# Modulation vectors from unsplit f32 weights in column tiles, and the loops written out

## The chip, the core and the metric

One core of one Trainium2 chip runs the whole kernel. Its engines work side by side and meet at semaphores: TensorE (PE, matmuls; PEld is its weight load), VectorE (DVE), ScalarE (ACT), GpSimd (POOL) and SyncE (SP), which issues all DMAs of this kernel. The metric is the device time of one execution in microseconds (us), lower is better.

## The reference

A two-layer backbone on 256 tokens of `x` and 256 context tokens, width 1024, all in f32. Each layer is FFN, mixer (window attention and gated linear attention), FFN. Each of the three is scaled, shifted and gated by modulation vectors, nine per layer, which depend on the condition alone:

```python
def adaln(cond, w, b):
    m = (cond @ w + b)[..., None, :]
    return jnp.split(m, N_MOD, axis=-1)          # N_MOD = 9, w is 1024 x 9216 per layer
def modulate(h, shift, scale):
    return h * (1 + scale) + shift
def swiglu(h, w13, w2):
    up, gate = jnp.split(h @ w13, 2, axis=-1)
    return (jax.nn.silu(gate) * up) @ w2

cond = jax.nn.silu(c)
cond_ctx = jax.nn.silu(c_ctx)
xc = ctx
for l in range(DEPTH):                           # DEPTH = 2
    m = adaln(cond, w_mod[l], b_mod[l])
    mc = adaln(cond_ctx, w_mod[l], b_mod[l])
    x = x + 0.5 * m[2] * swiglu(modulate(rmsnorm(x, norm_w[l, 0]), m[0], m[1]), ffn1_w13[l], ffn1_w2[l])
    xc = xc + 0.5 * mc[2] * swiglu(modulate(rmsnorm(xc, norm_w[l, 0]), mc[0], mc[1]), ffn1_w13[l], ffn1_w2[l])
    ...                                          # the mixer with m[3], m[4], m[5]
    x = x + 0.5 * m[8] * swiglu(modulate(rmsnorm(x, norm_w[l, 2]), m[6], m[7]), ffn2_w13[l], ffn2_w2[l])
    ...                                          # the context the same, in layer 0 alone
return x
```

So `adaln` is a product of two condition vectors (`c` and `c_ctx`) with two matrices of 1024 x 9216: 72 MB of weights for two result rows.

## The kernel before

Activations lie transposed: 8 row tiles `kt` of 128 features, 512 tokens side by side (256 in the last FFN). TensorE's fast form takes f32 data whose low bits are cut off (F32R). To keep f32 accuracy every operand is split into a high and a low part, and each product is made of three matmuls: high by high, high by low, low by high (`mm3`, L1248 to L1250).

Weights come in units of 1 MB. For each unit SP loads `raw` (two slots), ACT casts it into `WH` (L513, two halves), DVE subtracts to get `WL` (L823, two halves; this is `prep` on either engine), and PE uses it. `raw`, `WH` and `WL` have two slots each, so the split of unit n+2 waits until PE is through with unit n (`half_done`). Units are numbered in one order for all engines (`schedule`), and each unit is 48 matmuls of 512 columns where it belongs to an FFN.

The modulation vectors go through the same stream of units: 72 units of 256 columns (`unit_mod`, L1298 and L1299: the stationary operand `cst` is 128 columns wide and holds silu(c) and silu(c_ctx) with their low parts in four of them, the moving one is `WH` or `WL`, 256 columns; 16 matmuls a unit). DVE copies the four rows to `mrow` (L849), PE turns them into columns and adds high and low parts in one (`mod_turn`, L1311, a small f32 matmul by `hilo`), and DVE adds the bias (L854). Eight of the units stand ahead of everything. The others are spread over the first three FFNs by `FFN_SEGMENTS`: in FFN 0 three iterations with 4 units each and eight with 2, in FFN 1 eleven with 2, in FFN 2 seven with 2 and four with none. An iteration is two FFN units (one pair of `w13` tiles each, 22 in an FFN), and each such segment is a hardware loop.

After the 22 units of an FFN's first half come 11 units of its second half (`ffn_out`), which need the last gated product. Ahead of each FFN stands a norm: ACT squares, PE sums by a plain f32 matmul with `ones` (L1333), POOL multiplies by `rstd` (L460), DVE scales and shifts (L907), ACT casts to `hH`, DVE makes `hL` (L899), and the first FFN unit takes the eight tiles as they come.

A matmul of plain f32 operands (L1311, L1333, L1486) is written once in the code and runs as two matmul instructions, so the trace counts two for each. The trace names the tiles by the program's names: `PS` is PSUM, `hidH` and `hidL` the hidden state of an FFN, `sg` the gated product.

Of the kernel before, what the change touches and what calls it, by code (L numbers as in the profile page):

```python
# [13 lines left out]
P = 128  # L23
# [24 lines left out]
MOD_UNITS = N_MOD * D // UW  # L48
MOD_FIRST = 8
PAIR_AT = 2  # L50
MOD_GROUP = 4

FFN_SEGMENTS = [[(3, 4), (8, 2)], [(11, 2)], [(7, 2), (4, 0)], [(11, 0)]]


def schedule():
# [7 lines left out]

    take("mod", MOD_FIRST)
    for l in range(DEPTH):
        for j in range(2):
            k = 2 * l + j
            if j == 1:
                take(("attn_proj", l), 6)  # L70
                take(("branch_a", l), 8)
                take(("gla_proj", l), 1 + 2 * (2 + 4))
                take(("branch_g", l), 8)
                take(("out", l), 4)
            for s, (iters, fill) in enumerate(FFN_SEGMENTS[k]):
                take(("ffn_in", k, s), iters * (2 + fill))
            take(("ffn_out", k), GROUPS)
# [5 lines left out]
N_UNITS = START["end"]  # L83


def hybrid_backbone(nc, a, out):

    ctx = ExitStack()
    with ctx:
# [13 lines left out]
        WL = sb("WL", [P, 2, UN], F32R)  # L103
        mod = sb("mod", [P, DEPTH * N_MOD * KT, 2])
# [20 lines left out]
        mrow = sb("mrow", [P, MOD_GROUP, UW])  # L125
        rstd = mrow[:, 2:4, :].rearrange("p a c -> p (a c)")
# [62 lines left out]
        cst_hi = sem("cst_hi")  # L189
        cst_ready = sem("cst_ready")  # L190
# [4 lines left out]
        hilo_ready = sem("hilo_ready")  # L195
# [88 lines left out]
        wmod_d = [a["w_mod"][l].rearrange("(k p) c -> p k c", p=P) for l in range(DEPTH)]  # L284
# [60 lines left out]
        def _(sp):  # L345
# [10 lines left out]
            def load(n, slot, view, shape, pair=0):  # L356


                if pair == 0 and not (isinstance(n, int) and n < 2):
                    sp.wait_ge(lo_ready, 2 * n - 2)  # L360
                if pair == 1:
                    sp.wait_ge(lo_ready, 2 * n)
                dst = raw[:, slot, :].rearrange("p (k c) -> p k c", k=shape)
                sp.dma_start(dst, view).then_inc(raw_in[slot], 16)

            def load_pair(n, slot, f, view, at):

                sp.wait_ge(lo_ready, 2 * n - 2)
                dst = raw[:, slot, :].rearrange("p (k e c) -> p e k c", k=KT, e=2)
                sp.dma_start(dst[:, 0], view[:, :, 0:D_FF][:, :, bass.ds(at, P)]).then_inc(raw_in[slot], 16)  # L370
                sp.dma_start(dst[:, 1], view[:, :, D_FF:2 * D_FF][:, :, bass.ds(at, P)]).then_inc(gate_in[f], 16)

            load(0, 0, wmod_d[0][:, :, 0:UW], KT)
            load(1, 1, wmod_d[0][:, :, UW:2 * UW], KT)

# [7 lines left out]
            with sp.Fori(1, MOD_FIRST // 2) as i:  # L383
                for s in range(2):
                    load(2 * i + s, s, wmod_d[0][:, :, bass.ds(sp.snap((2 * i + s) * UW), UW)], KT)
# [9 lines left out]
            for k in range(4):  # L395
                l = k // 2
                if k % 2 == 1:
                    n = START[("attn_proj", l)]
                    cols = [COL["av"], COL["ak"]] + [COL["aq"] + j * UW for j in range(4)]
                    for j, c in enumerate(cols):  # L400
                        load(n + j, (n + j) % 2, win_d[l][:, :, c:c + UW], KT)
                    n = START[("branch_a", l)]
                    with sp.Fori(0, 4) as i:
                        load(n + 2 * i, n % 2, win_d[l][:, :, bass.ds(sp.snap(COL["ga"] + i * UW), UW)], KT, 1)
                        load(n + 2 * i + 1, (n + 1) % 2, wba_d[l][:, :, bass.ds(sp.snap(i * UW), UW)], KT, 2)
# [7 lines left out]
                    for j, c in enumerate(cols):  # L413
                        load(n + j, (n + j) % 2, win_d[l][:, :, c:c + UW], KT)
                    n = START[("branch_g", l)]
                    with sp.Fori(0, 4) as i:
                        load(n + 2 * i, n % 2, win_d[l][:, :, bass.ds(sp.snap(COL["gg"] + i * UW), UW)], KT, 1)
                        load(n + 2 * i + 1, (n + 1) % 2, wbg_d[l][:, :, bass.ds(sp.snap(i * UW), UW)], KT, 2)
                    n = START[("out", l)]
                    with sp.Fori(0, 2) as i:  # L420
                        for s in range(2):
                            load(n + 2 * i + s, (n + s) % 2, wout_d[l][:, :, bass.ds(sp.snap((2 * i + s) * UW), UW)], KT)
                g0 = 0
# [1244 lines left out]
```

## Time and profile before

| what | us |
|---|---|
| median of 3 runs (lowest to highest) | 2851.77 (2848.77 to 2857.4) |
| span of the profiled execution | 2850.1 |
| PE busy | 2542.8 (89%) |
| PEld busy | 2140.0 (75%) |
| DVE busy | 1278.3 (45%) |
| ACT busy | 1010.5 (35%) |
| POOL busy | 263.1 (9%) |
| mean granted TensorE clock | 0.958 of full |

A matmul's recorded time includes its way through the array, so neighbours overlap in the record; the distance from one start to the next is what it costs. 301.2 MB are moved. Times in the rows are us from the start of the span.

### The profile page before, as it was taken

The numbers are of one execution on the slowest core, as the hardware profiler recorded it, in microseconds if no ns is written. First come the engines' busy times: TensorE is split into PE (matmuls) and PEld (weight loads), VectorE is DVE, ScalarE is ACT, GpSimd is POOL, SyncE is SP. The second block draws the span as 40 slices with busy tenths as digits, with TensorE's granted clock in tenths as the row PEclk, the third lists the DMA queues.
The fourth block names the chain that finished last, engine by engine and source line by source line (L and its number), as shares of the span: only waits on it lengthen the run. The fifth ranks groups of instructions, "written<-read, shape, count | busy, mean of one in ns | idle before, by whom it ended". The sixth has DMA issues, their size and how long they took to land.

```text
span 2850.1 us, 34522 instructions
## 1 busy us (share of the span) xinstructions
PE 2542.8 (89%) x13357; PEld 2140.0 (75%) x13357; DVE 1278.3 (45%) x1675; ACT 1010.5 (35%) x1361; POOL 263.1 (9%) x296
## 2 busy tenths in 40 slices
PE   5999999896898887979999998999998788879999
PEld 4778778684777675857788786878786687779998
DVE  4544441436425544345444325443314654555554
ACT  3433331234324443233333213333213544454442
POOL 2000000100004533010000001000001002430000
PEclk8999999898999998989999999999998999999999
DMA  5554442120131101314444322444321142215564
GB/s 193 170 155 145 149 134 102 59 74 1 59 109 40 47 28 59 103 59 132 147 147 147 118 91 86 147 147 118 98 93 59 45 134 74 74 35 172 148 187 136
DMA packets 353492, 301.21 MB, mean 106 GB/s; under 512 B 6368, under 2 KB 341192, under 8 KB 353416
## 3 DMA queue, kind: packets, MB, share of 16 engines
q1 hardware_dynamic: 353416, 300.18, 34.3%
q8 instruction: 50, 0.82, 0.1%
q14 instruction: 26, 0.21, 0.0%
HBM read 299.10 MB, written 1.05 MB: 105 GB/s over the span
## 4 chain that ended last, share of the span: by engine, by line
PE 71%; DVE 12%; issue 6%; ACT 6%; POOL 3%; DMA 1%; SPq 0%; ACTq 0%; DVEq 0%; POOLq 0%
PE PS L1248 22%; PE PS L1250 20%; PE PS L1249 20%; DVE WL L823 4%; ACT WH L513 2%; DVE sq L907 2%; PE PS L1575 1%; PE PS L1311 1%; PE PS L1333 1%; POOL dq L469 1%; DVE hL L899 1%; PE PS L1536 1%; POOL dq L484 1%; DVE small L1039 1%; ACT dq L732 1%
## 5 line engine op out<-in xcount | busy, mean ns | idle before, releaser
L823 DVE TENSOR_TENSOR WL<-raw,WH 128x1024 fp32r<-128x1024 f32 x564 | 680.8, 1248 | 883.9 <-ACT WH L513 882.3
L513 ACT CAST WH<-raw 128x1024 fp32r<-128x1024 f32 x564 | 562.2, 1046 | 913.8 <-PE PS L1250 848.3
L1248 PE MATMUL PS<-hH,WH 128*128 128x512 f32 (+1 forms) x2096 | 780.7, 372 | 82.4 <-DVE WL L823 57.1
L1250 PE MATMUL PS<-hH,WL 128*128 128x512 f32 (+1 forms) x2096 | 758.1, 362 | 0.0
L1249 PE MATMUL PS<-hL,WH 128*128 128x512 f32 (+1 forms) x2096 | 758.1, 362 | 0.0
L1248 PEld LDWEIGHTS PS<-hH,WH 128*128 128x128 f32 x2096 | 402.8, 192 | 165.9 <-DVE WL L823 69.1
L1250 PEld LDWEIGHTS PS<-hH,WL 128*128 128x128 f32 x2096 | 403.3, 192 | 59.5
L1249 PEld LDWEIGHTS PS<-hL,WH 128*128 128x128 f32 x2096 | 404.1, 193 | 53.9 <-issue 1.0
L1248 PE MATMUL PS<-hidH,WH 128*128 (+2 forms) x704 | 260.0, 369 | 5.2 <-DVE sg L961 5.2
L1249 PE MATMUL PS<-hidL,WH 128*128 (+2 forms) x704 | 257.9, 366 | 0.0
L1250 PE MATMUL PS<-hidH,WL 128*128 (+2 forms) x704 | 257.0, 365 | 0.0
L460 POOL TENSOR_TENSOR sq<-xT,mrow 128x512 f32<-128x512 f32 (+1 forms) x48 | 65.9, 1407 | 1675.9 <-ACT mrow L547 1675.9
L1298 PE MATMUL PS<-WH,cst 128*128 128x256 f32 x576 | 149.5, 295 | 11.5 <-DVE WL L823 10.1
L1248 PEld LDWEIGHTS PS<-hidH,WH 128*128 128x128 f32 x704 | 132.0, 188 | 30.3 <-DVE sg L961 6.6
L1250 PEld LDWEIGHTS PS<-hidH,WL 128*128 128x128 f32 x704 | 132.6, 188 | 25.2
L1249 PEld LDWEIGHTS PS<-hidL,WH 128*128 128x128 f32 x704 | 132.2, 188 | 23.1
L1299 PE MATMUL PS<-WL,cst 128*128 128x256 f32 x576 | 145.4, 289 | 0.0
L1248 PE MATMUL PS<-actH,WH 128*128 128x512 f32 (+1 forms) x384 | 130.9, 341 | 13.5 <-DVE actL L1209 13.5
L1250 PE MATMUL PS<-actH,WL 128*128 128x512 f32 (+1 forms) x384 | 131.9, 343 | 0.0
L1249 PE MATMUL PS<-actL,WH 128*128 128x512 f32 (+1 forms) x384 | 131.3, 342 | 0.0
L1298 PEld LDWEIGHTS PS<-WH,cst 128*128 128x128 f32 x576 | 113.2, 197 | 18.3 <-DVE WL L823 13.3
L1283 PE MATMUL PS<-WH,hH 128*128 128x256 f32 x320 | 97.5, 305 | 26.0 <-DVE hL L899 26.0
(175 smaller groups left out, 2733.9 us busy)
## 6 DMA issues: line engine op xcount, KB each, us to landing
raw<-in_ffn_w SPq DMA_DIRECT2D x176, 512.0 KB, 4.6
raw<-in_w_mod SPq DMA_DIRECT2D x72, 1024.0 KB, 5.0
raw<-in_w_in SPq DMA_DIRECT2D x54, 1024.0 KB, 5.3
raw<-in_ffn_w SPq DMA_DIRECT2D x44, 1024.0 KB, 5.0
raw<-in_w_branch_attn SPq DMA_DIRECT2D x8, 1024.0 KB, 7.8
raw<-in_w_branch_gla SPq DMA_DIRECT2D x8, 1024.0 KB, 7.7
raw<-in_w_out SPq DMA_DIRECT2D x8, 1024.0 KB, 5.2
xin<-in_x SPq DMA_DIRECT2D x1, 1024.0 KB, 9.9
```

The lines of the kernel that those rows point to most:

```text
L460: nc.gpsimd.tensor_tensor(sq[:, kt, 0:T], xT[:, kt, 0:T], rstd[:, 0:T], ALU.mult).then_inc(xn_done, 1)
L469: ins = nc.gpsimd.tensor_tensor(dq[:, 0, d, :].rearrange("p (n m) -> p n m", m=P), b[:, :, at:at + 1].to_broadcast([P, NTB, P]), b, ALU.su ...
L484: nc.gpsimd.tensor_tensor(ov[:, 0, :, 0, :], fm, bv[:, 0, :, 0, :], ALU.subtract)
L513: nc.scalar.copy(half(WH, par, e, rows), half(raw, par, e, rows)).then_inc(hi_ready, 1)
L823: nc.vector.tensor_tensor(half(WL, par, e, rows), half(raw, par, e, rows), half(WH, par, e, rows).bitcast(F32), ALU.subtract).then_inc(lo_ ...
L907: ins = nc.vector.tensor_scalar(sq[:, kt, c * S:(c + 1) * S], sq[:, kt, c * S:(c + 1) * S], coefA[:, kt, c:c + 1], shift[:, kt, c:c + 1], ...
L1248: mm(o, wh, ah, start=start, stop=False)
L1249: mm(o, wh, al, start=False, stop=False)
L1250: return mm(o, wl, ah, start=False, stop=stop)
L1283: mm(o, ah, wh[:, kt, :], start=kt == 0, stop=False)
L1298: mm(PS[:, 4 + f, 0:UW], cst[:, kt, :], wh[:, kt, :], start=kt == 0, stop=False)
L1299: ins = mm(PS[:, 4 + f, 0:UW], cst[:, kt, :], wl[:, kt, :], start=False, stop=kt == KT - 1)
```

## The change

The modulation weights no longer pass through `raw`, `WH` and `WL`. They have two slots of their own (`mraw`, 128 x 2048), each filled by a row tile of 128 weight rows and 2048 columns (1 MB, a "piece", 72 in all; eight pieces, one for each `kt`, make a "set" of 2048 modulation values, nine sets). A piece is four plain f32 matmuls of 512 columns (`mod_piece`): the stationary operand is `cst[:, kt, :]`, 32 columns wide, and the result of column block j goes to PSUM partitions 32j to 32j+31, so each matmul uses another fourth of the array's columns. After eight pieces DVE copies the whole bank once (128 x 512) and PE turns it by four transposes; DVE adds the bias for 16 columns at once. Set 0 stands ahead of FFN 0. FFN 0 takes sets 1 to 3, FFN 1 sets 4 and 5, FFN 2 sets 6 to 8, a piece at a time between half units. Set 4 reaches over both layers and needs two DMAs a piece. `rstd` gets its own buffer. All hardware loops are written out, on all engines; the unit numbers become constants. Splits of the first pair of FFN 0 come ahead of the `kt` loop of the norm, those of FFN 1 to 3 in the stage before.

```diff
-FFN_SEGMENTS = [[(3, 4), (8, 2)], [(11, 2)], [(7, 2), (4, 0)], [(11, 0)]]
+MW = 2048
+MOD_SETS = DEPTH * N_MOD * D // MW
+MOD_Q = 4
+MOD_M = 32
+SETS_IN_FFN = [(1, 3), (4, 2), (6, 3), (9, 0)]
...
+def mod_places(k):
+
+    first, sets = SETS_IN_FFN[k]
+    places = {}
+    for i in range(KT * sets):
+        places.setdefault(i * (2 * FT - 3) // (KT * sets - 1), []).append(KT * first + i)
+    return places
...
+        mraw = sb("mraw", [P, 2, MW])
...
-        cst = sb("cst", [P, KT, P], F32R)
-        hilo = sb("hilo", [4, 2])
+        cst = sb("cst", [P, KT, MOD_M])
...
+            def load_mod(p):
+
+                kt, w = p % KT, MW // MOD_Q
+                if p >= 2:
+                    sp.wait_ge(mod_mm, p - 1)
+                for l in range(DEPTH):
+                    own = [(j, c) for j, (of, c) in enumerate(MOD_D[p]) if of == l]
+                    if own:
+                        (j0, c0), n = own[0], len(own)
+                        sp.dma_start(mraw[:, p % 2, j0 * w:(j0 + n) * w],
+                                     a["w_mod"][l][kt * P:(kt + 1) * P, c0 * w:(c0 + n) * w]).then_inc(mraw_in[p % 2], 16)
...
+            for p in range(2, KT):
+                load_mod(p)
+                if p >= KT - 2:
+                    f = p - KT + 2
+                    load_pair(START[("ffn_in", 0)] + f, f, w13_d[0])
...
+                for f in range(FT + 2):
+                    if f < FT:
+                        if k or f >= 2:
+                            load_pair(n + f, f, w13_d[k])
+                    else:
+                        load(w2 + f - FT, w2_d[k][:, 2 * (f - FT):2 * (f - FT) + 2, :], 2)
+                    if f >= 2:
+                        for at in (2 * f - 4, 2 * f - 3):
+                            for p in places.get(at, ()):
+                                load_mod(p)
...
+            def mod_rows(u):
+
+                dve.wait_ge(mod_mm, KT * (u + 1))
+                nc.vector.tensor_copy(mrow[:], PS[:, 4, :]).then_inc(mod_row, 1)
...
-            def unit_mod(n, f, par):
-
-                wh, wl = weights(par)
-                for e in range(2):
-                    pe.wait_ge(lo_ready, 2 * n + e + 1)
-                    for kt in range(e * KT // 2, (e + 1) * KT // 2):
-                        mm(PS[:, 4 + f, 0:UW], cst[:, kt, :], wh[:, kt, :], start=kt == 0, stop=False)
-                        ins = mm(PS[:, 4 + f, 0:UW], cst[:, kt, :], wl[:, kt, :], start=False, stop=kt == KT - 1)
-                    ins.then_inc(half_done, 1)
+            def mod_piece(p):
+
+                u, kt = divmod(p, KT)
+                w = MW // MOD_Q
+                pe.wait_ge(mraw_in[p % 2], mod_in(p))
+                if kt == 0 and u:
+                    pe.wait_ge(mod_row, u)
+                for j in range(MOD_Q):
+                    ins = mm(PS[j * MOD_M:(j + 1) * MOD_M, 4, 0:w], cst[:, kt, :], mraw[:, p % 2, j * w:(j + 1) * w],
+                             start=kt == 0, stop=kt == KT - 1)
+                ins.then_inc(mod_mm, 1)
...
+            def mod_turn(u):
+
+                pe.wait_ge(mod_row, u + 1)
+                if u:
+                    pe.wait_ge(mod_done, u)
+                for q in range(MW // MOD_Q // P):
+                    ins = nc.tensor.transpose(PS[:, 5, q * P:(q + 1) * P], mrow[:, q * P:(q + 1) * P], ident[:])
                 ins.then_inc(mod_t, 1)
...
-                    with pe.Fori(0, iters) as i:
...
+                for f in range(FT):
+                    if f > 1:
+                        pe.wait_ge((gated_a, gated_b)[f % 2], g0 + f // 2)
+                    unit_cols(n + f, 2 + f % 2, hH, hL, T, step=-2, h0=KT * ffn_norm(k) if f == 0 else None,
+                              between=[nothing] * 3 + [lambda: mods_at(2 * f)] + [nothing] * 3)
+                    mods_at(2 * f + 1)
+                    if f - 1 in ends:
+                        mod_turn(ends[f - 1])
...
-                pe.wait_ge(mod_done, GROUPS0[(k + 1, 0)] if k < 3 else GROUPS0["end"])
...
+                pe.wait_ge(mod_done, sum(SETS_IN_FFN[k]))
```

PE at the start of the program. `xin` is the input, `ident` and `ones` are constants. Before, the loop of the first modulation units follows the norm's sums:

```order
L1328 MATMUL PS<-ident,xin 128x128 x32
L1333 MATMUL PS<-sq,ones 128x512 x8
L1342 UNCONDITIONAL_BRANCH
L1296 ISA
L1298 MATMUL PS<-WH,cst 128x256
L1299 MATMUL PS<-WL,cst 128x256
```

Now:

```order
L1230 MATMUL PS<-ident,xin 128x128 x32
L1235 MATMUL PS<-sq,ones 128x512 x8
L1200 MATMUL PS<-mraw,cst 32x512 x32
L1213 MATMUL PS<-ident,mrow 128x128 x4
L1150 MATMUL PS<-hH,WH 128x512
```

The eight pieces of set 0 are 32 matmuls in a row, and the first FFN unit follows the transposes.

SP at the same place, behind the small constants. Before, the loop of modulation units, with two of them and the two halves of a pair in the FFN's loop:

```order
L382 DMA negsink<-in_attn_sink 128x16
L383 UNCONDITIONAL_BRANCH
L383 ISA
L364 ISA
L364 DMA raw<-in_w_mod 128x8x256
```

Now:

```order
L390 DMA negsink<-in_attn_sink 128x16
L378 DMA mraw<-in_w_mod 128x2048 x5
L366 DMA raw<-in_ffn_w 128x8x128
L367 DMA raw<-in_ffn_w 128x8x128
L378 DMA mraw<-in_w_mod 128x2048
L366 DMA raw<-in_ffn_w 128x8x128
L367 DMA raw<-in_ffn_w 128x8x128
```

The first pair of `w13` is issued behind the load of piece 6, and the last piece of set 0 behind that pair.

DVE at the end of FFN 0's first half. Before:

```order
L954 TENSOR_TENSOR sg<-sg,PS 128x512
L854 TENSOR_TENSOR mod<-PS,bmodT 128x8
L823 TENSOR_TENSOR WL<-raw,WH 128x1024 x2
L961 TENSOR_TENSOR sg<-sg,PS 128x512
L963 TENSOR_TENSOR hidL<-sg,hidH 128x1024
```

Now:

```order
L797 COPY mrow<-PS 128x512
L776 TENSOR_TENSOR WL<-raw,WH 128x1024 x2
L873 TENSOR_TENSOR sg<-sg,PS 128x512
L875 TENSOR_TENSOR hidL<-sg,hidH 128x1024
L803 TENSOR_TENSOR mod<-PS,bmodT 128x32
L776 TENSOR_TENSOR WL<-raw,WH 128x1024 x20
```

The last bias addition of the FFN moved behind the last gated product and its low part; `ffn_out` on PE waits for it.

## Rows read from the trace of the kernel before

**Rows 1.** The page: engines, and the chain that ended last

```profile
PE 2542.8 (89%) x13357; PEld 2140.0 (75%) x13357; DVE 1278.3 (45%) x1675; ACT 1010.5 (35%) x1361; POOL 263.1 (9%) x296
PE 71%; DVE 12%; issue 6%; ACT 6%; POOL 3%; DMA 1%; SPq 0%; ACTq 0%; DVEq 0%; POOLq 0%
```

**Rows 2.** Stretches: length, then busy us (instructions) by engine, PE clock, DMA

```profile
core 0: us, PE busy (x) PEld busy (x) DVE busy (x) ACT busy (x) POOL busy (x), PEclk, DMA share, GB/s
...
82.08:420.92 338.84, 319.26 (x1585) 264.43 (x1585) 157.29 (x187) 120.65 (x136) 0.00 (x0) 0.98 0.50 152
...
1272.39:1284.80 12.41, 2.45 (x18) 2.01 (x17) 9.00 (x7) 4.45 (x6) 10.37 (x8) 0.72 0.00 0
1284.80:1301.54 16.74, 14.35 (x48) 9.92 (x49) 13.03 (x23) 7.00 (x9) 1.08 (x1) 0.80 0.27 75
1272.39:1603.11 330.72, 304.67 (x1499) 251.75 (x1497) 153.85 (x177) 114.76 (x132) 11.46 (x8) 0.98 0.46 140
1732.87:2036.52 303.65, 282.30 (x1339) 232.70 (x1337) 132.58 (x149) 99.60 (x116) 11.45 (x8) 0.98 0.42 124
219.75:248.29 28.54, 27.36 (x137) 22.82 (x136) 12.54 (x14) 9.82 (x11) 0.00 (x0) 1.00 0.49 147
116.61:151.05 34.44, 32.92 (x177) 27.73 (x176) 17.84 (x20) 13.98 (x15) 0.00 (x0) 1.00 0.60 183
1939.61:2034.95 95.34, 95.34 (x421) 78.75 (x420) 31.36 (x31) 24.13 (x28) 0.00 (x0) 1.00 0.36 106
```

**Rows 3.** Timeline of PE, one modulation unit in FFN 0: start, us, instruction

```profile
219.51 0.40 PE L1250 MATMUL PS<-hH,WL 128*128 128x512 f32 x1
219.75 0.28 PE L1298 MATMUL PS<-WH,cst 128*128 128x256 f32 x1
219.87 0.28 PE L1299 MATMUL PS<-WL,cst 128*128 128x256 f32 x1
...
222.39 0.50 PE L1248 MATMUL PS<-hH,WH 128*128 128x512 f32 x1 [0.59 <-DVE WL L823]
```

**Rows 4.** Timelines of PE: plain f32 matmuls, the first with all columns, then row tiles

```profile
23.40 7.03 PE L1333 MATMUL PS<-sq,ones 128*128 128x512 f32 x16
...
6.29 0.30 PE L1320 MATMUL PS<-ident,rows 24*128 24x24 f32 x1
6.29 0.28 PE L1321 MATMUL PS<-ident,rows 16*128 16x16 f32 x1
...
851.73 0.39 PE L1250 MATMUL PS<-hH,WL 128*128 128x512 f32 x1
852.05 1.98 PE L1486 MATMUL PS<-lrT,gw 32*128 32x512 f32 x4
853.96 0.50 PE L1248 MATMUL PS<-hH,WH 128*128 128x512 f32 x1
```

**Rows 5.** Timeline of PEld in the norm's sums: weight loads of plain f32 matmuls

```profile
23.84 0.19 PEld L1333 LDWEIGHTS PS<-sq,ones 128*128 128x128 f32 x1 [0.24 <-ACT sq L543]
24.26 0.19 PEld L1333 LDWEIGHTS PS<-sq,ones 128*128 128x128 f32 x1 [0.24 <-issue]
```

**Rows 6.** The start: waits from 0 to 82 us; first FFN matmul; transposes; a PSUM copy

```profile
ACT WH L513 <- DMA raw<-in_w_mod: 20.2, 6, 6.3
...
82.08 0.50 PE L1248 MATMUL PS<-hH,WH 128*128 128x512 f32 x1 [0.75 <-DVE WL L823]
...
18.18 5.38 PE L1328 MATMUL PS<-ident,xin 128*128 128x128 f32 x32 [11.60 <-DMA xin<-in_ctx]
...
19.34 0.69 DVE L840 COPY xT<-PS 128x512 f32<-128x512 f32 x1 [5.87 <-PE PS L1328]
```

**Rows 7.** DMA: the page's queue row, and issues with KB and us to landing

```profile
q1 hardware_dynamic: 353416, 300.18, 34.3%
...
raw<-in_w_mod SPq DMA_DIRECT2D x72, 1024.0 KB, 5.0
```

**Rows 8.** Timelines of PE and DVE from FFN 0's first half to `ffn_out`

```profile
419.12 0.39 PE L1250 MATMUL PS<-hH,WL 128*128 128x512 f32 x1
420.92 0.49 PE L1248 MATMUL PS<-hidH,WH 128*128 128x512 f32 x1 [1.41 <-DVE sg L961]
...
420.18 0.69 DVE L961 TENSOR_TENSOR sg<-sg,PS 128x512 f32<-128x512 f32 x1 [6.58 <-ACT sg L590]
421.98 1.23 DVE L963 TENSOR_TENSOR hidL<-sg,hidH 128x1024 fp32r<-128x1024 f32 x1 [1.11 <-ACT hidH L592]
```

**Rows 9.** Timeline of PE: a norm with no modulation unit behind its sums

```profile
544.22 7.03 PE L1333 MATMUL PS<-sq,ones 128*128 128x512 f32 x16
560.97 0.55 PE L1283 MATMUL PS<-WH,hH 128*128 128x256 f32 x1 [9.73 <-DVE hL L899]
```

More of the change, by code:

```diff
@@ L437, in _ @@
-                n = START[("ffn_out", k)]
-                with sp.Fori(0, GROUPS // 2) as i:
-                    for s in range(2):
-                        load(n + 2 * i + s, (n + s) % 2, w2_d[k][:, bass.ds(sp.snap((2 * i + s) * 2), 2), :], 2)
-                load(n + GROUPS - 1, (n + GROUPS - 1) % 2, w2_d[k][:, FT - 2:FT, :], 2)
+                    for j in range(4):
+                        load(n + j, wout_d[l][:, :, j * UW:(j + 1) * UW])
+                n, places = START[("ffn_in", k)], mod_places(k)
@@ L443, in _ @@
+                for g in range(2, GROUPS):
+                    load(w2 + g, w2_d[k][:, 2 * g:2 * g + 2, :], 2)
             sp.wait_ge(out_ready, 2)
@@ new lines, in ffn @@
+                n = START[("ffn_in", k)]
+                for i in range(GROUPS):
+                    u, g = n + 2 * i, g0 + i
+                    prep(u + 1)
+                    act.wait_ge(half_done, 2 * (u + 1))
+                    if g:
+                        act.wait_ge(hid_lo, g)
+                    nc.scalar.activation(sg[:, 0, 0:T], PS[:, 0, 0:T], ACT.Silu).then_inc(silu_done, 1)
+                    prep(u + 2, rows=i == GROUPS - 1)
+                    act.wait_ge(half_done, 2 * (u + 2))
+                    nc.scalar.activation(sg[:, 1, 0:T], PS[:, 1, 0:T], ACT.Silu).then_inc(silu_done, 1)
+                    act.wait_ge(gated_b, g + 1)
+                    nc.scalar.copy(hidH[:, 2 * i:2 * i + 2, 0:T], sg[:, :, 0:T]).then_inc(hid_hi, 1)
@@ L604, in ffn @@
                 n = START[("ffn_out", k)]
-                with act.Fori(0, GROUPS // 2) as i:
-                    for s in range(2):
-                        prep(n + 2 * i + s + 1, (n + s + 1) % 2, rows=True)
-                prep(n + GROUPS, (n + GROUPS) % 2, rows=k == 1)
+                for g in range(GROUPS):
+                    prep(n + g + 1, rows=g < GROUPS - 1)
             def qk_tiles(l, j):
@@ L683, in branch @@
                 nc.scalar.preload_act_table(ACT.Sigmoid)
[L684 to L685 removed]
+                for i in range(4):
+                    prep(n + 2 * i + 1)
                     act.wait_ge(half_done, 2 * (n + 2 * i + 1))
```

442 lines of the change are left out of this document (141 added, 301 removed).

## The prediction

> **What bounds the kernel now.** I read the page first: PE is busy for 89% of the span and holds 71% of the chain that ended last, DVE and ACT are busy for 45% and 35% [rows 1]. So time goes where PE's own stream gets shorter or longer, and work taken from DVE and ACT counts only where PE waits for it. Then I cut the span into stretches [rows 2]. The last four iterations of FFN 2 carry no modulation unit: 420 matmuls of 512 columns in 95.3 us, 0.227 each, so an FFN unit of 48 costs 10.9 and an iteration of two 21.8. An iteration with two modulation units takes 28.54 and one with four 34.44. The two units of the first therefore cost 6.7: each is 16 matmuls at 0.12 (1.9), then PE stands 0.6 for the low part of the next weights, because a modulation unit is shorter on PE than its successor's split on ACT and DVE; from the first of the 16 to the next FFN matmul it is 2.64 [rows 3]. Twice 2.64 and a turn of 1.06 and the loop's end make up the rest. The start is bound otherwise: the first FFN matmul comes at 82.08, and until there ACT waits 20.2 us for modulation weights [rows 6].
>
> **The change, by stretches.** Modulation touches PE in four places: the start, and FFN 0, 1 and 2. Of the profiled execution these are 0 to 420.92, 1272.39 to 1603.11 and 1732.87 to 2036.52, each up to the first matmul of `ffn_out` [rows 2, 8]: 420.9 + 330.7 + 303.7 = 1055.3 us. I build the same three anew, with c for what one piece costs PE.
>
> *The price c of a piece.* It is four plain f32 matmuls of 512 columns. Such a matmul shows as two instructions, and 16 of them take 7.03 us: 0.43 each, 0.86 for one matmul as written [rows 4]. No row shows column tiles. The bounds:
> Serial, all eight instructions one after the other: 8 x 0.43 = 3.44.
> All four tiles side by side: two instructions deep, 0.86.
> Between them: rows show that different tiles of the array can run together, since L1320 and L1321, in row tiles at rows 64 and 0, start within the same 0.01 us [rows 4]. But the instructions come tile by tile, and the second of a tile cannot stream before its first is through; if PE starts matmuls in program order, the first instruction of tile j+1 starts with the second of tile j, and the piece takes five slots: 5 x 0.43 = 2.15.
> Weight loads lie under the preceding matmul: 0.19 in a slot of 0.43, with 0.24 idle [rows 5]. Changing the tile shape costs extra: four instructions in a 32-row tile take 852.05 to 853.96, 1.91 for 1.72 of streaming, and start 0.1 late [rows 4]; with the slow second matmul behind it I take 0.4 a piece.
> So c is 1.3, 2.55 or 3.84. I take the middle one, rounded to 2.6, since the rows that are nearest (L1320, L1321) show tiles together and every row shows PE starting in order. That is the decisive choice of this prediction: 64 pieces lie in the FFNs, and each 0.1 us of c is 6.4 us.
>
> The Trainium skill, "TensorE: Matmul & The Clock Gate", section "Part 3: Packing small matmuls — row/col tiling", gives 2.38 times the speed for three column tiles and says that matmuls start and end strictly in program order. The first figure alone would carry over as about 0.8 of full overlap, an estimate by that page of 1.1 us a piece and some 2711 us in all; the second is the reason for five slots. The same section says that a weight load overlaps a running matmul only where the row groups differ, which all four tiles here share. The trace speaks against that for full tiles [rows 5], and no run so far shows it for column tiles; it is the fourth case below.
>
> *Start.* PE sums the norm until 30.3 (23.40 and 16 slots of 0.43) [rows 4]. Pieces 0 and 1 have landed by then and run to 35.5. The other six go through two slots: a load of 1 MB lands 5.0 us after issue [rows 7], so a round of two pieces takes about 5.0 + 2.6 + 0.5, and three rounds with the last piece end near 59. The pair of FFN 0 is issued between pieces 6 and 7; the queue moved 300 MB in 34.3% of the span, 3.4 us per MB [rows 7], so piece 7 ends near 62. Then in a chain: copy of the bank 0.7 (L840 has the same shape) [rows 6], four transposes 0.7 (32 took 5.38), bias and coefficients 0.5, DVE's split of the first pair 2.4, and scale, cast and low part of the first tile with their semaphores 3. First FFN matmul at 70, against 82.1; bounds 62 (loads fully side by side) and 78.
>
> *First unit of an FFN.* It takes the eight tiles as they come, partly at the lower clock: 16.7 us in FFN 1 (1284.80 to 1301.54, clock 0.80) [rows 2]. I keep 16.7 for all three; between 14 and 20.
>
> *Norm ahead of FFN 1 and 2.* 12.4 us from the end of the sums to the first matmul, with a modulation unit on PE inside and the split of a modulation unit on DVE in front of the scaling [rows 2]. Without either it is like the norm of the mixer: sums start at 544.22, the last of 16 starts 15 x 0.43 later, at 550.7, and the first matmul comes at 560.97, 10.3 later [rows 9]. Saves 2.1 each.
>
> *Stream.* 21 units x 10.9 = 228.9 in each FFN. The 2.64 and 1.06 of the old units are gone. In their place 24c, 16c and 24c, and turns of 0.7 inside the stream (2, 1 and 2). A piece follows its set's DVE copy where it begins the next set: the copy comes up to 4.9 us after a unit's end, the piece 5.5 after it, so it is just covered; if not, 1 us a set.
>
> *Into `ffn_out`.* Now PE resumes 1.8 us after its last matmul started, released by the gated product [rows 8]. The bias addition now stands behind the cast and the low part, which ends at 423.21, and PE waits for it: 4.5 instead of 1.8. I add 2 for the clock, since a pause of that length can bring half rate for a stretch. Between 2.5 and 9 an FFN.
>
> *Covered at nothing:* the 1 MB loads of pieces inside the FFNs (a piece is issued about 1.5 units, 15 us, ahead; a landing takes 5.0; the DMA share was 0.36 to 0.60 in those stretches [rows 2] and the bytes stay the same); SP's in-order wait for a piece's slot ahead of the next pair (the piece two before is done a unit earlier); 72 splits fewer on ACT and DVE; the loops written out. That last has one exposed piece, at most 2 us in all: branches at loops' ends in the mixer. FFN 3, the mixers and the `ffn_out` parts are as before.
>
> *Sum,* in us: FFN 0 with the start: 70 + 16.7 + 228.9 + 1.4 + 4.5 + 2 + 24 x 2.6 = 385.9. FFN 1: 10.3 + 16.7 + 228.9 + 0.7 + 4.5 + 2 + 16 x 2.6 = 304.7. FFN 2: 10.3 + 16.7 + 228.9 + 1.4 + 4.5 + 2 + 24 x 2.6 = 326.2. Together 1016.8 against 1055.3: 38.5 less. FFN 0 gains 35, FFN 1 26, and FFN 2 loses 22, since it carries 24 pieces where 14 units stood. Span 2850.1 - 38.5 = 2811.6; the median of the runs is 1.7 above the profiled span, so 2813. In general the gain is 275 less the start less 64c; even is reached at c = 3.2.
>
> **Rivals.**
> *All four tiles together,* c = 1.3, start at 65: gain 127, 2725 us. For it: tiles that start in the same 0.01 us [rows 4]. Against it: two instructions of one tile stand next to each other in the stream.
> *Serial,* c = 3.84, start at 75: 46 us slower, 2898. It decides as soon as a column tile's matmul waits for the one before it, for instance because f32 operands in two instructions, or another input path of the array, don't allow two streams. For it: no row shows two matmuls of 512 columns side by side. It loses although nothing stalls: 64 x 3.84 is 246 us of PE for what cost some 215 with its waits.
> *Serial with open weight loads,* each instruction 0.43 + 0.19: c = 5.4, start at 82, about 3000.
> *The new waits eat the gain:* c = 2.6, but each DVE copy, each bias addition and each pause costs its upper bound: 9 sets x 1, 3 x 4.5 more, first units at 20, start at 78: 40 us back, 2853, no change.
>
> **Numbers.** A change under 0.3%, 9 us, can't be told from none. Five slots 0.47, around 2813 with its own range 2785 to 2840 (c from 2.3 to 2.9, and the start). All together 0.20, serial 0.22, serial with open loads 0.04, waits eat the gain 0.07. Faster by over 0.3% (under 2843): 0.20 + 0.45 = 0.65; same 0.08; slower 0.27. The range takes in the all-together and the serial case, 2715 to 2905.
>
> **What would show it.** In the trace after, four matmul groups on `mraw`: starts of the eight instructions of a piece at 0, 0.43, 0.43, 0.86, 0.86 and so on for five slots, pairwise for all together, 0.43 apart throughout for serial. From the last FFN matmul before a piece to the first one behind it: 2.6 + 0.2. First FFN matmul near 70. `ffn_out` released by the bias addition after 4.5, three times. FFN 2 longer than before by 22. An idle PE ahead of pieces, released by the load of `mraw`, would show my cover for the loads wrong; one ahead of FFN matmuls with no releaser would put it on the written-out code.

## The result, and the profile after

| | before | changed | ratio |
|---|---|---|---|
| median, us | 2850.81 (2848.77 to 2857.4) | 2703.19 (2699.01 to 2704.76) | 0.947 (95% interval 0.9458 to 0.9481) |
| profiled span, us | 2850.1 | 2702.8 | |

147.6 us less, where 38 less was forecast: outside the range, whose lower end was 2715. It is the case "all four tiles together" (2725) and some 20 us more.

The page of the changed kernel, engines and chain:

```profile
PE 2427.4 (90%) x12529; PEld 1976.6 (73%) x12529; DVE 1088.5 (40%) x1444; ACT 871.4 (32%) x1216; POOL 253.1 (9%) x296
PE 76%; DVE 10%; issue 6%; ACT 4%; POOL 3%; DMA 1%; SPq 0%; DVEq 0%; POOLq 0%; ACTq 0%
```

PE has 115 us less to do and was nearly as large a share of the span before [rows 1]: the kernel is still bound there, and its own stream got shorter. DVE and ACT have 190 and 139 us less, which hardly counts by itself.

Stretches of the changed kernel (columns as in [rows 2]): the start; FFN 0 from its first matmul to `ffn_out`; FFN 1 and FFN 2 from the end of the norm's sums to `ffn_out`; 90 us of `ffn_out`.

```profile
0.00:64.41 64.41, 28.06 (x122) 11.36 (x122) 12.04 (x25) 12.25 (x17) 11.28 (x16) 0.77 0.63 217
64.41:341.83 277.42, 273.39 (x1260) 202.38 (x1261) 89.67 (x103) 72.90 (x86) 0.00 (x0) 0.99 0.54 178
1187.74:1467.33 279.59, 264.34 (x1194) 201.58 (x1193) 97.88 (x106) 75.45 (x90) 10.52 (x8) 0.98 0.44 139
1595.19:1884.80 289.61, 274.42 (x1263) 202.13 (x1261) 98.48 (x108) 75.45 (x90) 10.52 (x8) 0.98 0.49 160
350.00:440.00 90.00, 90.00 (x399) 74.53 (x398) 18.88 (x16) 16.03 (x16) 0.00 (x0) 1.00 0.28 94
```

The three stretches of the sum are now 64.4 + 277.4 + 279.6 + 289.6 = 911.0 against 1055.3: 144.3 of the 147.3 us between the two spans. FFN 0 with the start gained 79.1, FFN 1 51.1 and FFN 2 14.0, which the forecast had losing 22.

Now the piece itself. Timelines of PE: three narrow windows on the first piece (each row groups the instructions that are under way in the window; its first number is the first start, the last the count), then a piece between FFN matmuls, and under it the weight loads (PEld) there.

```profile
29.55 0.64 PE L1200 MATMUL PS<-mraw,cst 128*32 128x512 f32 x4
...
29.55 1.07 PE L1200 MATMUL PS<-mraw,cst 128*32 128x512 f32 x8
...
30.00 1.04 PE L1200 MATMUL PS<-mraw,cst 128*32 128x512 f32 x8
...
73.16 0.40 PE L1152 MATMUL PS<-hH,WL 128*128 128x512 f32 x1
73.48 1.06 PE L1200 MATMUL PS<-mraw,cst 128*32 128x512 f32 x8
74.48 0.50 PE L1150 MATMUL PS<-hH,WH 128*128 128x512 f32 x1
...
73.48 0.16 PEld L1200 LDWEIGHTS PS<-mraw,cst 128*32 128x32 f32 x8 [0.37 <-issue]
```

Four instructions start at 29.55, in the window 29.54 to 29.70, and four more from 30.00 on; the next piece follows at 30.43. So it is pairs in four tiles: two slots of 0.43 for eight instructions, 0.88 a piece, where one plain matmul alone already takes 0.86 [rows 4]. The four starts of a slot lie 7 ns apart. The rows do not name the tile of an instruction; that one of each tile starts at once is read from the number four and from the run with one tile, below, where no two instructions start together. All eight weight loads lie within 0.16 us, under the first slot. In the stream PE goes from its last FFN matmul to the next in 1.32 us. That is 1.09 beside the matmul's own 0.227, and the 48 matmuls behind a piece begin a little slower. A whole period is the safest measure: with one piece to a unit of 48, PE resumes at 93.29 and again at 105.39.

```profile
93.29 0.50 PE L1150 MATMUL PS<-hH,WH 128*128 128x512 f32 x1
...
105.39 0.50 PE L1150 MATMUL PS<-hH,WH 128*128 128x512 f32 x1
```

12.10 less 48 x 0.227 gives c = 1.20: the number to set against the forecast's 2.6.

The start, and the step into `ffn_out` (timelines of PE, then of DVE):

```profile
35.55 1.08 PE L1200 MATMUL PS<-mraw,cst 128*32 128x512 f32 x4 [4.08 <-DMA mraw<-in_w_mod]
...
36.41 1.08 PE L1200 MATMUL PS<-mraw,cst 128*32 128x512 f32 x4
...
55.54 1.93 PE L1200 MATMUL PS<-mraw,cst 128*32 128x512 f32 x8 [4.15 <-DMA mraw<-in_w_mod]
58.29 1.12 PE L1213 MATMUL PS<-ident,mrow 128*128 128x128 f32 x4 [0.81 <-DVE mrow L797]
64.41 0.77 PE L1150 MATMUL PS<-hH,WH 128*128 128x512 f32 x1 [5.00 <-DVE hL L826]
...
337.55 0.39 PE L1152 MATMUL PS<-hH,WL 128*128 128x512 f32 x1
337.78 0.60 PE L1213 MATMUL PS<-ident,mrow 128*128 128x128 f32 x4
341.83 0.64 PE L1150 MATMUL PS<-hidH,WH 128*128 128x512 f32 x1 [3.46 <-issue]
...
338.61 0.69 DVE L873 TENSOR_TENSOR sg<-sg,PS 128x512 f32<-128x512 f32 x1 [8.55 <-ACT sg L556]
340.40 1.23 DVE L875 TENSOR_TENSOR hidL<-sg,hidH 128x1024 fp32r<-128x1024 f32 x1 [1.11 <-ACT hidH L558]
341.55 0.18 DVE L803 TENSOR_TENSOR mod<-PS,bmodT 128x32 f32<-128x32 f32 x1
```

Two stretches of the same start (columns as in [rows 2]), and what PE waits for on pieces, up to 65 us and in the whole kernel (us in total, times, longest):

```profile
35.50:57.50 22.00, 11.61 (x48) 1.22 (x48) 0.00 (x0) 1.99 (x2) 5.41 (x5) 0.50 0.93 311
57.50:64.41 6.91, 1.12 (x5) 0.75 (x5) 5.55 (x11) 1.24 (x2) 0.00 (x0) 0.50 0.22 56
...
PE PS L1200 <- DMA mraw<-in_w_mod: 14.4, 6, 4.2
...
PE PS L1200 <- DMA mraw<-in_w_mod: 14.7, 7, 4.2
```

At the start PE waits for the load of each of pieces 2 to 7, and these six run at a granted clock of 0.50: the second four instructions of a piece start 0.86 behind the first four (35.55 and 36.41), not 0.43, so a piece takes 1.7 us there. Inside the FFNs the loads are covered, as forecast: 14.4 of the 14.7 us of waits stand at the start.

Into `ffn_out` PE resumes 4.28 us after its last FFN matmul, against 1.80 [rows 8], in the order that the forecast gave: gated product, cast, low part (L875), bias (L803, ends at 341.73), and then PE. The trace names no releaser there, only "issue"; that it is the bias addition is read from the 0.1 us between the two rows and borne out by the run without it below.

### The profile page after: what moved, and what is told of

Same layout as the page of the kernel before. It is cut to its first block, busy times and chain, and to the rows that moved or that the text cites. A ratio compares the mean times of both kernels' runs of the same rounds, so it can differ in the third digit from the quotient of the medians.

```text
span 2702.8 us, 29281 instructions
## 1 busy us (share of the span) xinstructions
PE 2427.4 (90%) x12529; PEld 1976.6 (73%) x12529; DVE 1088.5 (40%) x1444; ACT 871.4 (32%) x1216; POOL 253.1 (9%) x296
## 4 chain that ended last, share of the span: by engine, by line
PE 76%; DVE 10%; issue 6%; ACT 4%; POOL 3%; DMA 1%; SPq 0%; DVEq 0%; POOLq 0%; ACTq 0%
PE PS L1150 22%; PE PS L1151 22%; PE PS L1152 22%; PE PS L1200 3%; DVE sq L833 2%; PE PS L1458 1%; PE PS L1235 1%; POOL dq L473 1%; DVE hL L826 1%; DMA mraw<-in_w_mod 1%; DVE WL L776 1%; PE PS L1419 1%; DVE small L941 1%; ACT dq L685 1%; POOL dq L488 1%
## 5 line engine op out<-in xcount | busy, mean ns | idle before, releaser
L776 DVE TENSOR_TENSOR WL<-raw,WH 128x1024 fp32r<-128x1024 f32 x420 | 502.7, 1238 | 531.4 <-ACT WH L516 530.7
L516 ACT CAST WH<-raw 128x1024 fp32r<-128x1024 f32 x420 | 418.9, 1046 | 457.2 <-PE PS L1152 417.3
L1150 PE MATMUL PS<-hidH,WH 128*128 128x512 f32 (+1 forms) x704 | 257.5, 366 | 11.3 <-issue 10.4
L1151 PE MATMUL PS<-hidL,WH 128*128 128x512 f32 (+1 forms) x704 | 257.3, 365 | 0.0
L1152 PE MATMUL PS<-hidH,WL 128*128 128x512 f32 (+1 forms) x704 | 257.0, 365 | 0.0
L464 POOL TENSOR_TENSOR sq<-xT,rstd 128x512 f32<-128x512 f32 (+1 forms) x48 | 57.9, 1240 | 1533.3 <-ACT rstd L533 1533.3
L873 DVE TENSOR_TENSOR sg<-sg,PS 128x512 f32<-128x512 f32 (+1 forms) x44 | 27.3, 621 | 314.5 <-ACT sg L556 314.5
L556 ACT ACTIVATE sg<-PS 128x512 f32<-128x512 f32 (+1 forms) x44 | 23.9, 544 | 354.1 <-PE PS L1152 354.1
L869 DVE TENSOR_TENSOR sg<-sg,PS 128x512 f32<-128x512 f32 (+1 forms) x44 | 27.3, 620 | 231.4 <-ACT sg L553 231.4
```

What stands on the lines that cost most here:

```text
L464: nc.gpsimd.tensor_tensor(sq[:, kt, 0:T], xT[:, kt, 0:T], rstd[:, 0:T], ALU.mult).then_inc(xn_done, 1)
L516: nc.scalar.copy(half(WH, n % 2, e, rows), half(raw, n % 2, e, rows)).then_inc(hi_ready, 1)
L776: nc.vector.tensor_tensor(half(WL, n % 2, e, rows), half(raw, n % 2, e, rows), half(WH, n % 2, e, rows).bitcast(F32), ALU.subtract).then_i ...
L869: nc.vector.tensor_tensor(sg[:, 0, 0:T], sg[:, 0, 0:T], PS[:, 2, 0:T], ALU.mult).then_inc(gated_a, 1)
L873: nc.vector.tensor_tensor(sg[:, 1, 0:T], sg[:, 1, 0:T], PS[:, 3, 0:T], ALU.mult).then_inc(gated_b, 1)
L1150: mm(o, wh, ah, start=start, stop=False)
```

## Experiments

Periods and c below are read as above, from one PE resumption behind a piece to the next, with 48 FFN matmuls between them. The kernel before was timed anew beside each group of runs, with medians of 2854.8, 2854.0 and 2854.7; the ratios are to those. The changed kernel was not timed again. Its 2703.2 stands beside a 2850.8 of the kernel before, so differences to it in microseconds are sure to some 4 us only.

**One column tile for all four.** The four matmuls of a piece write the same 32 partitions, into one sum; three quarters of the modulation vectors get no sum of their own.

```
-  mm(PS[j * MOD_M:(j + 1) * MOD_M, 4, 0:w], ...
+  mm(PS[0:MOD_M, 4, 0:w], ...
```

> The changed kernel with one edit: all four matmuls of a piece write PSUM partitions 0 to 31, so they share one column tile instead of having one each. Instructions, shapes and bytes are the same; the modulation vectors come out wrong (the four column blocks are added up). Theory (the four column tiles stream side by side, and that alone makes a piece cheap): the eight instructions run one after the other, 8 x 0.43 = 3.44 a piece, some 2.55 more than now; 64 pieces in the FFNs make 163 us, the eight at the start some 12 of which the loads hide a part: 2870 to 2885 in all, slower than the kernel before. Rival (a piece is cheap because it needs no split and no wait, the tiles matter little): under 2760.

Measured 2871.09 us (2869.2 to 2871.96), ratio 1.0054 (1.0038 to 1.0071): slower than before the change. PE, the first two instructions of a piece, and a period:

```profile
82.86 0.62 PE L1200 MATMUL PS<-mraw,cst 128*32 128x512 f32 x1
...
83.32 0.59 PE L1200 MATMUL PS<-mraw,cst 128*32 128x512 f32 x1
...
124.94 0.50 PE L1150 MATMUL PS<-hH,WH 128*128 128x512 f32 x1
...
139.59 0.50 PE L1150 MATMUL PS<-hH,WH 128*128 128x512 f32 x1
```

The instructions start one by one. 14.65 less 10.90 is c = 3.75, the serial case of the forecast (3.84). With the same 72 pieces, transfers, waits and written-out loops the kernel is 16 us slower than before when the tiles don't run side by side, and 147 faster when they do. The column tiles are worth 168 us (2871.1 - 2703.2), more than the whole gain.

**Halves, tile by tile.** Each of the four matmuls is cut into two of 256 columns that stand next to each other in the program, in the same tile.

```
   for j in range(MOD_Q):
+      for e in range(2):
+          ... columns e * w // 2 to (e + 1) * w // 2 of tile j
```

> The changed kernel with each of a piece's four matmuls cut into two of 256 columns, written tile by tile: both of tile 0, both of tile 1, and so on. 16 instructions a piece instead of 8, the same columns in all. Theory A (TensorE doesn't hold a tile's matmul back for one of another tile that is still waiting, whatever the program order): a piece stays near 0.9 plus 0.2, the whole within 10 us of the changed kernel, 2703 to 2713. Theory B (matmuls start in program order, and only the two passes of one f32 matmul are taken apart): tile j+1 starts with the second half of tile j, five slots of 0.43, about 2.15 plus 0.2 a piece, 1.2 x 64 = 80 us more: about 2783.

Measured 2703.37 us (2700.35 to 2705.47), ratio 0.947 (0.9454 to 0.9486): the same as the changed kernel. The window 30.25 to 30.35 and a period:

```profile
30.26 0.44 PE L1201 MATMUL PS<-mraw,cst 128*32 128x256 f32 x4
...
82.07 0.50 PE L1150 MATMUL PS<-hH,WH 128*128 128x512 f32 x1
...
94.23 0.50 PE L1150 MATMUL PS<-hH,WH 128*128 128x512 f32 x1
```

Each tile now has four instructions of its own in a row, and still one of each of the four tiles starts at once; c is 1.26. A tile's second instruction, as the kernel writes them, therefore does not hold back another tile's first. (Whether PE itself takes them out of the written order, or they reach it so, no row shows.) That ends "five slots": with order kept, this form would have taken 13 slots of 0.22, 2.8 us.

**Only one of the four matmuls,** in all pieces but the first of each set.

```
   for j in range(MOD_Q):
+      if j and kt:
+          continue
```

> The changed kernel, where in 63 of the 72 pieces (all but the first of each set) only the first of the four matmuls stands, and the other three column tiles get nothing; three quarters of the modulation vectors are then wrong from there on, and every transfer, wait and turn stands as it was. 56 of the 64 pieces in the FFN stretches are cut so. Theory A (the four column tiles run beside each other, and three of the four matmuls cost only their issue, some 7 ns each in the trace of the changed kernel): 1 us less, 2702 us (2699 to 2704). Theory B (the four share the engine, so that each is a quarter of the 0.86 us): 56 x 0.65 = 36 us less, 2667.

Measured 2699.1 us (2692.98 to 2699.47), ratio 0.9452 (0.9436 to 0.9468). PE resumes at 124.00 and 136.09: c = 1.19 with one matmul, 1.20 with four.

```profile
124.00 0.50 PE L1150 MATMUL PS<-hH,WH 128*128 128x512 f32 x1
...
136.09 0.50 PE L1150 MATMUL PS<-hH,WH 128*128 128x512 f32 x1
```

The period gives 0.6 us in all for the three left out. The 4 us of the medians are more than that, and not explained by it. How far traces differ where nothing was edited shows in the second layer's mixer. This run leaves it as the changed kernel has it, and the change altered only its loops and where its buffers lie. From the last of its norm's sums to the first of the next norm's, in the kernel before, the changed kernel and this one:

```profile
2166.25:2637.25 471.00, 389.29 (x2578) 353.49 (x2577) 255.67 (x397) 211.71 (x336) 84.85 (x128) 0.93 0.28 86
...
2012.64:2489.82 477.18, 397.61 (x2578) 358.78 (x2577) 255.66 (x397) 210.86 (x336) 88.38 (x128) 0.91 0.27 85
...
2012.00:2479.12 467.12, 392.19 (x2578) 356.96 (x2577) 255.53 (x397) 210.73 (x336) 83.81 (x128) 0.92 0.28 87
```

Of the 11.6 us between the profiled runs of the last two, 10.1 stand there. The 36 us of "each a quarter" are excluded.

**Every piece's four matmuls twice.**

```
+  for r in range(2):
       for j in range(MOD_Q):
```

> The changed kernel, where each piece issues its four matmuls twice in a row, into the same sums (the modulation vectors come out twice as large). In the changed kernel a piece makes the stream of FFN matmuls 1.09 us longer, of which two passes of 512 columns are 0.88 us by the pieces that follow one another at the start. Theory A (1.09 is 0.88 for the passes, paid again, and 0.21 for going over to the other shape and back, paid once): 64 x 0.88 = 56 us more, 2759 us (2755 to 2763), and the gap in the stream is 2.2 us a piece. Theory B (the 1.09 goes with each set of four): 64 x 1.09 = 70 us more, 2773.

Measured 2759.03 us (2755.79 to 2759.21), ratio 0.9658 (0.964 to 0.9675); 56 us more, as the first theory had it. The period:

```profile
131.00 0.50 PE L1150 MATMUL PS<-hH,WH 128*128 128x512 f32 x1
...
144.00 0.50 PE L1150 MATMUL PS<-hH,WH 128*128 128x512 f32 x1
```

13.00, c = 2.10. The second set costs 0.90, so 0.3 of the 1.20 goes to changing the shape and back and is paid once, however many matmuls stand in the piece. Two pieces in one place would save some 0.3 us, 32 such pairs 10 us; that was not run.

**The kernel before, with its loops written out.** Only every loop of the program was unrolled, with constants as addresses and wait values.

```
-  with pe.Fori(0, iters) as i:
+  for i in range(0, iters):
```

> The kernel before with all its hardware loops written out on all engines, and nothing else changed: the modulation units are split and interleaved as before. Theory (the loops' share is what the two traces show outside the modulation): ffn_out's matmuls at 0.227 instead of 0.233, 3 x 3.5 us, and 5 us at the branch loops' ends and in their matmuls, 1 us more in the last FFN: 16 to 20 us less than before, 2831 to 2835. Rival 1 (written-out code costs nothing and gives nothing, as forecast): 2849 to 2851. Rival 2 (the 0.6 us stands ahead of FFN units were the loops' register work, not the splits): 30 us or more less.

Measured 2857.88 us (2854.05 to 2863.41), ratio 1.0011 (1.0001 to 1.0022). The theory fell: written-out loops give nothing. That agrees with the forecast's "at most 2 us", but it left a question open, since `ffn_out`, which the change does not touch, ran faster. Stretches of 90 us in `ffn_out`, of the kernel before and of this one:

```profile
440.00:530.00 90.00, 90.00 (x388) 72.39 (x387) 18.90 (x16) 16.00 (x16) 0.00 (x0) 1.00 0.28 95
...
440.00:530.00 90.00, 90.00 (x387) 72.41 (x386) 18.88 (x16) 16.01 (x16) 0.00 (x0) 1.00 0.28 96
```

388 and 387 matmuls of 512 columns in 90 us, 0.232 each, at full clock in all; the changed kernel has 399, 0.226 each (first block of rows after). Loops don't explain it.

**Where the buffers lie.** In the kernel before, `hidH`, `hidL`, `actH` and `actL` begin 32 bytes off a multiple of 64 in each partition, by the sizes of the buffers ahead of them; the change drops and adds other buffers ahead of them, and they now begin at a multiple of 64. One run moves them back in the changed kernel, the other moves them down in the kernel before.

```
+  pad = sb("pad", [P, 8])
   with ExitStack() as r:
       below_sq = ...
```

> The changed kernel with 32 unused bytes ahead of hidH, hidL, actH and actL, which then begin 32 bytes off a multiple of 64, as in the kernel before. Theory A: the pitch in ffn_out rises from 227 to 231-237 ns and the time by 14 us to 2717 (2713 to 2721); then some 14 us of the 148 gained come from where the buffers lie and 134 from the column tiles and what goes with them. Theory B: 2703 as before.

Measured 2712.81 us (2707.8 to 2714.83), ratio 0.9499 (0.9476 to 0.9521): 9.6 more than the changed kernel, or 8 by the ratios. Its `ffn_out`, then that of the other run:

```profile
350.00:440.00 90.00, 90.00 (x387) 72.29 (x386) 18.88 (x16) 16.02 (x16) 0.00 (x0) 1.00 0.26 86
...
440.00:530.00 90.00, 90.00 (x395) 73.86 (x394) 20.94 (x18) 17.99 (x18) 0.00 (x0) 1.00 0.28 93
```

```
-  hilo = sb("hilo", [4, 2])
-  epsc = sb("epsc", [P, 2])
+  epsc = sb("epsc", [P, 4])
+  hilo = epsc[0:4, 2:4]
```

> The kernel before, with the two numbers of hilo put into free room of epsc, so that every buffer behind lies 32 bytes lower: hidH, hidL, actH and actL then begin at multiples of 64 bytes as in the changed kernel, where they began 32 bytes off in the kernel before. Theory A (a plain 256-column matmul reads its moving operand 5 to 9 ns slower when it begins 32 bytes off): 1582 matmuls with hid by 6.5 ns and 578 with act by 6.5 ns, together 14 us, so 2837 us (2833 to 2841), and the pitch in ffn_out falls from 231-237 to 227 ns. Theory B (the pitch comes from something else that the change brought, such as the loops or the traffic of the queue): the pitch stays at 231 to 237 ns and the time at 2851 (2848 to 2855).

Measured 2843.42 us (2837.22 to 2849.39), ratio 0.996 (0.9948 to 0.9973): 11 us less than before, from where a buffer of 8 bytes stands. 32 empty bytes bring 399 matmuls down to 387; taking them out of the kernel before brings 388 up to 395, not to 399. So the address is shown to be a cause. It is worth some 10 us of the 147, where 14 were expected from the pitch (the distance from one start to the next); 9.6 and 11 carry an uncertainty of some 4 us each, and the firm evidence is the pitch. What keeps the last 4 in 90 us is open: in that kernel matmuls of the first kind (`hidH` with `WH`) are still 231 ns apart from the next, the other two kinds 228.

**The last piece of an FFN one unit earlier.** The pieces of a stage are spread over two half units fewer, so that copy, transposes and bias lie under the last unit.

```
-  places.setdefault(i * (2 * FT - 3) // (KT * sets - 1), [])
+  places.setdefault(i * (2 * FT - 5) // (KT * sets - 1), [])
```

> The changed kernel with the pieces of each FFN placed over 40 half units instead of 42, so that the last piece, the turn and the last bias addition come one unit earlier and ffn_out no longer waits for them. Theory (the pause ahead of ffn_out is 4.1 instead of 1.8 us and brings TensorE to half rate for a stretch behind it, 2.2 us): 3 x 4.5 = 13 us less, 2690. Rival (the half rate comes from the pause of 1.8 as well, or falls elsewhere): 3 x 2.35 = 7 less, 2696.

Measured 2689.74 us (2684.81 to 2692.15), ratio 0.9414 (0.9398 to 0.943): 13.5 less than the changed kernel. The step into `ffn_out` of FFN 0:

```profile
340.87 0.39 PE L1152 MATMUL PS<-hH,WL 128*128 128x512 f32 x1
342.67 0.50 PE L1150 MATMUL PS<-hidH,WH 128*128 128x512 f32 x1 [1.41 <-DVE sg L873]
343.01 0.39 PE L1151 MATMUL PS<-hidL,WH 128*128 128x512 f32 x1
343.24 0.40 PE L1152 MATMUL PS<-hidH,WL 128*128 128x512 f32 x1
```

1.80 again, released by the gated product as in [rows 8]; so it was the turn and its bias that held PE in the changed kernel. And the matmuls behind start 0.34, 0.23, 0.23 apart. In the changed kernel the granted clock of the stretch behind the pause is 0.61, some eight matmuls being 0.43 apart, half of the full rate, in each of the three FFNs (in FFN 1 a few matmuls later). Under its row, the same stretch of FFN 1 in the run with one of four matmuls:

```profile
341.83:346.20 4.37, 4.37 (x12) 3.46 (x13) 2.17 (x2) 0.44 (x1) 0.00 (x0) 0.61 0.26 46
...
1467.49:1471.90 4.41, 4.41 (x19) 3.64 (x20) 2.16 (x2) 0.43 (x1) 0.00 (x0) 1.00 0.21 49
```

The lower clock does not follow every such pause. Of the 21 pauses of 4.3 us in the seven traces that have them, 18 are followed by 6 to 14 slow matmuls and three by none, as in that row; of the 15 of 1.8 us in five traces none is.

Per FFN that is 2.1 for the pause (2.48 less 0.36 for the turn, which now lies in the stream) and 1.7 for the clock, 11 us in three; the 13.5 measured are that within the uncertainty.

**The first pairs ahead of pieces 2 to 7.** The queue carries them while the norm's sums run.

```
+  for f in range(2):
+      load_pair(START[("ffn_in", 0)] + f, f, w13_d[0])
   for p in range(2, KT):
       load_mod(p)
-      if p >= KT - 2: ... load_pair
```

and DVE splits the first pair ahead of the first set's rows, not between them and the scaling.

> The changed kernel, with the loads of the first two pairs of the FFN issued before pieces 2 to 7 of the start and not behind them. The queue then carries 2 MB in the stretch in which the norm sums run and it stands idle. In the changed kernel the queue issues nothing between its first loads and 30.7 us, and TensorE then waits 14.7 us in 7 waits for pieces of w_mod, while 6 MB of pieces and 2 MB of pairs share the queue. Theory A (what sets the start is the bytes that are still to come behind 30.7 us): 6 MB in place of 8 MB at the same rate, the first FFN matmul at 58 to 60 us against 64.4, the whole 2697 us (2695 to 2700). Theory B (the start is set by the two buffers of pieces, each reload waiting for its piece's matmuls, whatever else the queue holds): first FFN matmul at 63 to 65, the whole 2702 to 2704. Rival on the other side: the pairs delay pieces 2 and 3 by more than they give back, 2706 or more.

Measured 2694.17 us (2693.64 to 2697.71), ratio 0.9443 (0.9421 to 0.9464), 9.0 less. PE's start:

```profile
52.69 1.94 PE L1198 MATMUL PS<-mraw,cst 128*32 128x512 f32 x8 [1.10 <-DMA mraw<-in_w_mod]
55.44 1.12 PE L1211 MATMUL PS<-ident,mrow 128*128 128x128 f32 x4 [0.81 <-DVE mrow L796]
59.29 0.77 PE L1148 MATMUL PS<-hH,WH 128*128 128x512 f32 x1 [2.73 <-DVE hL L826]
```

The first FFN matmul comes at 59.29, not 64.41; 2.9 of the 5.1 are the pieces' (PE waits 11.3 us for them, not 14.4), 2.3 the wait for DVE's scaled tile, 2.73 and not 5.00, since the split of the pair is no longer in front of it. The expectation had named the bytes alone. The last piece still takes two slots of 0.86 (1.94 in the row). The time of the first FFN matmul swings from run to run by itself: in kernels with an unchanged start it is 64.4, 65.3 and 67.5 us.

**Both.**

> Both edits on the changed kernel: the last piece of a stage one unit earlier (measured alone: 2689.7 against 2703.2) and the pairs ahead of the pieces at the start. They stand in different stages, so the gains should add: 2684 us (2681 to 2687) by theory A of the other run, 2690 by theory B.

Measured 2682.22 us (2681.53 to 2682.93), ratio 0.9397 (0.9377 to 0.9418): 21.0 less than the changed kernel, 13.5 and 9.0 alone. It is the fastest here.

## Why the prediction was wrong, point by point

*What bounds the kernel: right.* Only what shortened PE's stream or its waits counted.

*The price c: wrong, and it is the miss.* The step that failed is "if PE starts matmuls in program order, the first instruction of tile j+1 starts with the second of tile j". The rows show four instructions starting within 0.02 us in the first slot of a piece and four in the second, and cutting the matmuls further tile by tile changed nothing. The row tiles of [rows 4] that start within 0.01 us had pointed the right way; "every row shows PE starting in order" was true of those rows, but none had two tiles with work enough to tell. The bounds held: 1.20 lies between 0.86 and 3.84, near the 1.3 of "all together", and serial came out at 3.75. Even the term for the change of shape was near, 0.3 measured for 0.4. 64 x 1.4 is 89.6 of the 110 us between forecast and result.

The Trainium skill, "TensorE: Matmul & The Clock Gate", section "Part 3: Packing small matmuls — row/col tiling", says that matmuls start and end strictly in program order, and that was the reason for five slots. For f32 matmuls, each of two instructions, in different column tiles the trace does not agree (four starts 7 ns apart, the next four 0.43 later). Its rule that a weight load overlaps a matmul only in another row group does not show here either: eight loads of the same row group lie within 0.16 us under the first slot. Its 2.38 for three tiles, from which the prediction had estimated some 2711 us, is what came closest to the 2703; the runs show 3.75 to 1.20 for four tiles with all that goes with them, 3.1 times.

The other terms, each against its own row (us):

| term | forecast | measured | adds to the miss |
|---|---|---|---|
| c, 64 pieces | 2.6 | 1.20 | 89.6 |
| first FFN matmul | 70 | 64.4 | 5.6 |
| first unit of FFN 0, 1, 2 | 16.7 | 14.9, 16.7, 16.7 | 1.8 |
| stream, 21 units | 228.9 | taken as forecast | 0 |
| turns in the stream, 5 | 0.7 | 0.4 | 1.5 |
| norm to first matmul, 2 | 10.3 | 10.3 | 0 |
| into `ffn_out`, 3 | 4.5 | 4.1 (4.28 less the last slot) | 1.2 |
| clock behind it, 3 | 2 | 1.7 | 0.9 |
| loops written out | 0 to 2 | nothing to be seen | 0 |
| where the buffers lie | not seen | 10 | 10 |

The first units are what is left of each FFN when 21 x 10.9, the pieces, the turns and the pause are taken from its stretch, for instance 269.3 - 228.9 - 19.2 - 0.4 - 4.1 = 16.7 in FFN 1 (from 1198.05). The terms sum to 110.6, where 109.8 is to be explained. So close a fit is partly luck: the buffers' 10 us come from separate runs, and between the two traces all that lies outside the three stretches gained only 3.0, since the second layer's mixer alone took 6.2 more (477.2 against 471.0, rows above). Why the mixers differ by several microseconds from trace to trace, in both directions, is open.

*The start:* right in its order, too dear in its rounds. The last piece ends at 57.5 and not at 62, and the chain behind it takes 6.9 and not 8. A round of two pieces takes about 7 us (PE starts pieces 2, 4 and 6 at 35.55, 42.39 and 49.46), where 8.1 was forecast. The 5.0 for the load was right: the first reload is issued at 30.68 and PE starts on it at 35.55. The other term, 2.6 for the piece, is 1.7 there. That is more than the 0.88 of the first two, since the granted clock is 0.50 in this stretch, which the forecast did not have. (The page gives 7.8 us to landing as the median of all 64 whole loads; most of them are in the FFNs.)

*Into `ffn_out`:* right in mechanism and near in size, shown by the run that moves the turn. The clock's share, 2 forecast and 1.7 measured, is of the right size where it falls, but it does not fall behind every such pause.

*Rivals:* "serial" was 27 us too dear as a whole (2898 against 2871 measured) though its c was right to 0.1; the buffers (10 us), c (64 x 0.09) and the turns, pauses and the start make the rest. Serial with open weight loads and "new waits" are refuted by the rows. No case had buffers' addresses in it, and 2715 as a lower end left no room below "all together": a case that stood at 0.20 had its neighbourhood cut off at 10 us.

## What to carry to other kernels

Here four plain f32 matmuls with a small stationary operand (32 columns), one in each column tile, cost the time of one, and that made plain f32 cheaper than splitting the weights on two other engines. But whether the tiles run side by side was worth 168 us here: where no row of a profile shows that, measure a piece alone first, or keep the range open on both sides. When a stage ends in a chain on other engines (copy, turn, bias), put its last piece a unit earlier, and look for the pause's second bill, the lower clock behind it. Write down where buffers begin before and after a change: 10 us came from 32 bytes.

## What the runs showed of the hardware

Four f32 matmuls of 128x32 by 128x512 in four column tiles: 0.88 us in a row of such pieces at full clock, 1.7 at a granted clock of 0.50, 1.20 between matmuls of 128x128, of which 0.3 is paid once for the change of shape (c of 1.20, 2.10 with two sets, 1.19 with one matmul alone).
Matmuls of 512 columns whose moving operand begins 32 bytes off a multiple of 64 start 0.232 apart, others 0.226 (387 and 399 in 90 us), both at a granted clock of 1.00. It shows in `hid` and, by about the same amount (0.227 and 0.233), in `act`.
After 18 of 21 pauses of 4.3 us, 6 to 14 matmuls ran 0.43 apart, at half the full rate (1.2 in place of 2.4 GHz); after 15 pauses of 1.8 us none did.
